# A two-layer hybrid decoder step on one core: running square sums in PSUM, unrolled residual loops, value pages loaded behind the output projection's weights

## The chip, the cores and the metric

The kernel runs on one core of a Trainium2 chip, in one launch. The metric is device time in microseconds (us). Before the change it is 1196.12 us, the median of three runs (1194.81 to 1197.56).

## The reference, cut to what matters

320 tokens (256 of a prompt, and 8 sequences of 8 new tokens) of width 1024 pass through two layers in float32. Cut to its core, a layer is:

```python
x = x + 0.5 * swiglu(rmsnorm(x, g1), w_gate1, w_up1, w_down1)      # 1024 -> 2816 -> 1024
z = rmsnorm(x, g) @ w_in                                           # 1024 -> 2048
q, k, v, p_in, c_in, d_in = split(z)
att  = moba_attention(q, concat(k_past, k), concat(v_past, v))     # past: pages picked by page_table
pool = pool_mixer(p_in)                                            # window means 2/4/8/16
conv = conv_module(c_in)                                           # GLU, depthwise 31, LayerNorm, swish
gmlp = spatial_gating(d_in)                                        # gelu, rmsnorm, causal mixing
x = x + concat(att, pool, conv, gmlp) @ w_out                      # 1024 -> 1024
x = x + 0.5 * swiglu(rmsnorm(x, g2), w_gate2, w_up2, w_down2)

def rmsnorm(x, gain):
    return x * rsqrt(mean(x * x, axis=-1) + 1e-6) * gain
```

The 8 sequences each have 256 past keys and values, two pages of 128 rows per sequence, whose place in the pool is read from `page_table` at run time.

## The kernel before

Channels lie on the 128 partitions and the 320 tokens along the free axis, so x is 8 tiles of 128 x 320 (`DT` = 8). Each weight is split into a rounded high part and a low rest, and so is each input; an output tile is the sum of three products (high by high, high by low, low by high), at lines L577, L578 and L580 of `use_slot`. For each input tile that is three matmuls of 128 x 128 by 320 columns.

The engines are programmed separately and meet at semaphores, in an order written out by hand. The outermost loop on each is over the two layers.

- **SyncE (SP)** issues the loads. Weights come in slots: four buffers `raw[j]`, each loaded at L347 (`load_slot`) once GpSimd has finished with its former content (semaphore `split`). In the input projection, SP waits until the FFN is done (its memory is reused), then goes through the last 8 of the 16 slots; behind each slot it loads the two pages of one sequence (`load_past`): per page it reads the page's number into a register, issues 128 KB of keys (L373) and 128 KB of values (L375). Both count on one semaphore, `kv_in`. Then come the 8 slots of the output projection, and those of the second FFN.
- **ScalarE (ACT)** rounds a slot to its high part `w_hi` (L885), as soon as it has landed and TensorE is done with the former slot in that place. In between it does the activations of the mixers, in a fixed order.
- **GpSimd (POOL)** subtracts to get the low part `w_lo` (L470). In the mixer stage, behind the last slot of the input projection, it also does the last 8 taps of the batch's convolution (`late_history_taps`, L488 and L491) and the sums of the pooling windows (`window_sums`, L506 to L533); only then it goes on to the slots of the output projection.
- **TensorE (PE)** runs the columns (24 matmuls, one output tile), and between the last columns of the input projection the small matmuls of the mixers. `batch_scores` (L700) reads the past keys and waits for `kv_in`; `batch_attention` (L787, L790), some 24 us later, reads the past values and has no wait for them of its own.
- **VectorE (DVE)** scales, does the taps of the convolution, the softmax's parts and all low parts of the inputs.

RMSNorm is applied late: the input of a matmul is x times the gain (`xg_hi` by ACT, L870; `xg_lo` by DVE, L1109), and the factor 1/rms multiplies the outputs. For it `residual` (L1151 on) does, for each of the 8 tiles of x: add the matmul's output to x (L1160), the low part `xg_lo` (L1109), and `add_square` (L1117), which adds the squares that ACT made (`square`, L877) to `sumsq` in SBUF. At the end one matmul with a matrix of ones (L620, `sum_squares`) sums over the partitions, ACT takes the root (L866), and `invert_norm` inverts it (L1121), sets `sumsq` to zero (L1122) and waits for its reciprocal. `residual` is a loop on the engine, of 2 tiles an iteration behind an FFN and of 4 behind the output projection. It runs three times a layer. Of the 8 PSUM banks, bank 7 holds the running sums of the convolution (`conv_sum`), later the conv statistics and one of the pooling maps.

Of the kernel before, what the change touches and what calls it, by code (L numbers as in the profile page):

```python
# [27 lines left out]
ALU = mybir.AluOpType  # L28
# [7 lines left out]
TOK = SEQ + NS  # L36
# [61 lines left out]
def hybrid_decoder(nc, xT, w8, w11, gains, vecs, consts, pool_w, conv_pw, sp_wT, sp_b,  # L98
# [3 lines left out]
    with ctx:  # L102
# [119 lines left out]
        kv_in = sig("kv_in", 16 * 2 * DEC_B * PAGES)  # L222
# [14 lines left out]
        summed = sig("summed", 3 * (DT + 1), DT + 1)  # L237
# [71 lines left out]

        conv_sum = bank[7][:, :].rearrange("p (c t) -> p c t", c=GT)  # L310
# [30 lines left out]
        def _(sp):  # L341
# [24 lines left out]
            def load_past(L, b):  # L366

                one = bass.ds(L, 1)
                for n in range(PAGES):
                    page = sp.value_load(page_row[0:1, bass.ds(b * PAGES + n, 1)],  # L370
                                         min_val=0, max_val=cache_v.shape[1] - 1)
                    at_page = bass.ds(page, 1)
                    sp.dma_start(k_all[:, :, bass.ds(b, 1), n * PAGE:(n + 1) * PAGE].rearrange("p c b t -> p c (b t)"),  # L373
                                 cache_kT[one, at_page, :, :, :].rearrange("l a p c t -> (l a p) c t")).then_inc(kv_in.sem, 16)
                    sp.dma_start(v_past[:, bass.ds(b * PAGES + n, 1), :].rearrange("p b t -> p (b t)"),  # L375
                                 cache_v[one, at_page, :, :].rearrange("l a p n -> (l a p) n")).then_inc(kv_in.sem, 16)
# [51 lines left out]
            with sp.Fori(0, DEPTH) as L:  # L428
# [10 lines left out]
                with sp.Fori(0, DEC_B // 4) as n:  # L439
                    for j in range(4):  # L440
                        load_slot(L, BASE_I, 2 + n, j, w8, L * W8_ROWS + (W8_I + 2) + n, HALVES8)
                        load_past(L, n * 4 + j)
                with sp.Fori(0, IT_O) as i:
                    load(L, BASE_O, i, w8, L * W8_ROWS + W8_O + i, HALVES8)
# [122 lines left out]
        def _(pe):  # L567
# [49 lines left out]
            def sum_squares(L, n):  # L617

                pe.wait_ge(summed.sem, L * summed.per + (n + 1) * (DT + 1))
# [72 lines left out]
            def batch_scores(L):  # L692
                pe.wait_ge(pads.sem, pads.at(L, 6))
                pe.wait_ge(kv_in.sem, kv_in.at(L, kv_in.per))
# [89 lines left out]
            def batch_attention(L):  # L784
                for g in range(2):
# [75 lines left out]
        def _(act):  # L861
# [69 lines left out]
            def norm_tile(L, tile0, norm, d, e):  # L931
                hold(act, taken.sem, L * taken.per + d + (tile0 + 1 + taken.head))
                norm_input(L * (3 * DT) + d + norm * DT, d, e, L * summed.per + d + norm * (DT + 1))
# [163 lines left out]
        def _(dve):  # L1097
# [16 lines left out]
            def add_square(squares, signal, tile_count, sum_count):  # L1114
                dve.wait_ge(signal.sem, tile_count + 1)
                dve.wait_ge(summed.sem, sum_count + 1)
                dve.tensor_tensor(sumsq[:, :], sumsq[:, :], squares, ALU.add).then_inc(summed.sem, 1)  # L1117

            def invert_norm(L, n):
                dve.wait_ge(norm_root.sem, norm_root.at(L, n + 1))  # L1120
                dve.reciprocal(rms[:, :], root[:, :]).then_inc(norm_ok.sem, 1)  # L1121
                dve.memset(sumsq[:, :], 0.0).then_inc(summed.sem, 1)  # L1122
# [28 lines left out]
            def residual(L, base, tile0, norm, factor, tiles_an_iteration, banks):  # L1151

                n_banks = len(banks)
# [384 lines left out]
```

## Time and profile before

| what | value |
|---|---|
| median of three runs | 1196.12 us (1194.81 to 1197.56) |
| the profiled execution | 1197.89 us, its span 1195.9 us |
| busy in the span | PE 1173.2 us (98%), DVE 623.4 us, ACT 547.8 us, POOL 814.4 us |
| mean granted TensorE clock | 0.995 of full speed |
| layer one, input projection and mixers | 245 to 339 us of the span |
| layer two, the same stage | 833 to 931 us of the span |

The profile is of one execution. "Busy" is the time in which an engine works on an instruction; matmuls overlap, one starts some 0.15 us after another and lasts 0.31 us, so PE's busy time shows where it stands still, and not how well it runs. The idle time in front of an instruction carries the name of what ended it. In the timeline that stands in square brackets; where there is none, the instruction followed at once.

### The profile page before, as it was taken

To read this page: it belongs to the slowest core of one execution; us is meant where nothing else is said; L and a number is where in the kernel's file an instruction comes from. 1 tells how busy PE (TensorE), PEld (TensorE's weight loads), DVE (VectorE), ACT (ScalarE), POOL (GpSimd) and SP (SyncE) were. 2 spreads that over 40 slices of the span, in tenths; PEclk is the share of its full clock that TensorE was granted. 3 is DMA by queue.
4 is the path that set the end of the run, shared out by engine and by line. 5 is a ranking of instruction groups with operands and counts; after the bars stand their busy time and mean duration, and the time that the engine had idled before them with its cause. 6 is when DMAs were issued, how large, how long until landed. Compare 5 with 4: busy or idle time off the path is not lost.

```text
span 1195.9 us, 24294 instructions
## 1 busy us (share of the span) xinstructions
PE 1173.2 (98%) x7924; PEld 1142.5 (96%) x7924; DVE 623.4 (52%) x913; ACT 547.8 (46%) x808; POOL 814.4 (68%) x427
## 2 busy tenths in 40 slices
PE   7999999999999999999999999999999999999998
PEld 6999999998789999999999999999986999999998
DVE  5775571247966444431157675522777664544212
ACT  5444444443845443444444444444455554443444
POOL 6776667675866767667767666677567566767677
PEclk9999999999999999999999999999998999999999
DMA  8454435566246544445555444455662364444455
GB/s 286 151 160 151 148 116 149 158 180 201 71 140 179 156 144 156 133 122 154 162 173 167 149 155 129 133 154 168 186 199 71 110 174 143 154 144 135 135 147 172
DMA packets 71831, 182.79 MB, mean 153 GB/s; under 512 B 10074, under 2 KB 24802, under 8 KB 71778
## 3 DMA queue, kind: packets, MB, share of 16 engines
q1 hardware_dynamic: 71488, 181.07, 49.7%
q10 hardware_dynamic: 290, 1.10, 0.2%
q8 instruction: 24, 0.39, 0.1%
q14 instruction: 29, 0.24, 0.1%
HBM read 178.55 MB, written 3.58 MB: 152 GB/s over the span
## 4 chain that ended last, share of the span: by engine, by line
PE 91%; DVE 5%; issue 1%; DMA 1%; ACT 1%; DVEq 0%; POOL 0%; SPq 0%; ACTq 0%
PE bank L577 29%; PE bank L580 29%; PE bank L578 29%; DVE xg_lo L1109 1%; DMA x<-in_xT 1%; DVE bank L1187 1%; PE bank L790 0%; PE bank L814 0%; PE bank L767 0%; DMA raw<-in_w 0%; PE bank L594 0%; PE bank L602 0%; PE bank L598 0%; PE bank L658 0%; DVE prob L1295 0%
## 5 line engine op out<-in xcount | busy, mean ns | idle before, releaser
L470 POOL TENSOR_TENSOR w_lo<-raw,w_hi 128x1024 fp32r<-128x1024 f32 (+2 forms) x353 | 767.7, 2179 | 360.3 <-ACT w_hi L885 360.1
L885 ACT ACTIVATE w_hi<-raw 128x1024 fp32r<-128x1024 f32 (+2 forms) x353 | 339.4, 962 | 471.0 <-PE bank L580 430.2
L577 PE MATMUL bank<-xg_hi,w_hi 128*128 128x320 f32 x1600 | 498.1, 311 | 5.1 <-DVE xg_lo L1109 4.2
L580 PE MATMUL bank<-xg_hi,w_lo 128*128 128x320 f32 x1600 | 494.9, 309 | 0.0
L578 PE MATMUL bank<-xg_lo,w_hi 128*128 128x320 f32 x1600 | 494.9, 309 | 0.0
L577 PEld LDWEIGHTS bank<-xg_hi,w_hi 128*128 128x128 f32 x1600 | 300.5, 188 | 10.0 <-DVE xg_lo L1109 5.3
L578 PEld LDWEIGHTS bank<-xg_lo,w_hi 128*128 128x128 f32 x1600 | 300.5, 188 | 0.6
L580 PEld LDWEIGHTS bank<-xg_hi,w_lo 128*128 128x128 f32 x1600 | 300.5, 188 | 0.0
L580 PE MATMUL bank<-h_hi,w_lo 128*128 128x320 f32 x704 | 217.8, 309 | 0.0
L577 PE MATMUL bank<-h_hi,w_hi 128*128 128x320 f32 x704 | 217.8, 309 | 0.0
L578 PE MATMUL bank<-h_lo,w_hi 128*128 128x320 f32 x704 | 217.8, 309 | 0.0
L1139 DVE TENSOR_TENSOR h_lo<-tmp,h_hi 128x320 f32 (+1 forms) x88 | 167.4, 1903 | 75.2 <-ACT h_hi L901 75.2
L577 PEld LDWEIGHTS bank<-h_hi,w_hi 128*128 128x128 f32 x704 | 132.2, 188 | 0.0
L578 PEld LDWEIGHTS bank<-h_lo,w_hi 128*128 128x128 f32 x704 | 132.2, 188 | 0.0
L580 PEld LDWEIGHTS bank<-h_hi,w_lo 128*128 128x128 f32 x704 | 132.2, 188 | 0.0
L1160 DVE SCALAR_TENSOR_TENSOR x<-bank,x 128x320 f32 x48 | 23.4, 487 | 203.1 <-PE bank L580 203.1
L1134 DVE TENSOR_TENSOR tmp<-bank,rms 128x320 f32<-128x320 f32 x88 | 43.1, 489 | 157.9 <-PE bank L580 157.8
L1109 DVE SCALAR_TENSOR_TENSOR xg_lo<-x,gain,xg_hi (+1 forms) x56 | 71.2, 1279 | 58.0 <-ACT xg_hi L870 58.0
L897 ACT ACTIVATE tmp<-tmp 128x320 f32<-128x320 f32 x88 | 40.7, 462 | 67.3 <-DVE tmp L1132 67.1
L1137 DVE TENSOR_TENSOR tmp<-tmp 128x320 f32<-128x320 f32 x88 | 57.3, 651 | 7.2 <-ACT tmp L897 4.7
L901 ACT ACTIVATE h_hi<-tmp 128x320 f32 (+1 forms) x88 | 41.5, 472 | 27.8 <-DVE tmp L1137 27.7
L1215 DVE SCALAR_TENSOR_TENSOR conv_y<-conv_in,vec,conv_y 128x64 f32<-128x64 f32 x88 | 46.7, 571 | 3.0
(180 smaller groups left out, 807.1 us busy)
## 6 DMA issues: line engine op xcount, KB each, us to landing
raw<-in_w SPq DMA_DIRECT2D x227, 512.0 KB, 3.8
raw<-in_w SPq DMA_DIRECT2D x64, 384.0 KB, 3.1
raw<-in_w SPq DMA_DIRECT2D x64, 320.0 KB, 2.9
k_all<-in_cache_kT SPq DMA_DIRECT2D x32, 128.0 KB, 2.9
v_past<-in_cache_v SPq DMA_DIRECT2D x32, 128.0 KB, 2.6
cst<-in_consts ACTq DMA_DIRECT2D x1, 997.0 KB
out_yT<-x SPq DMA_DIRECT2D x1, 960.0 KB, 7.4
x<-in_xT SPq DMA_DIRECT2D x2, 320.0 KB, 4.6
```

The source lines that it names most:

```text
L470: pool.tensor_tensor(w_lo[:, j, 0:count * P], raw[:, j, 0:count * P], w_hi[:, j, 0:count * P].bitcast(F32), ALU.subtract).then_inc(split.s ...
L577: pe.matmul(out, hi, in_hi[:, k, :], start=first and n == 0, stop=False)
L578: pe.matmul(out, hi, in_lo[:, k, :], start=False, stop=False)
L580: mm = pe.matmul(out, lo, in_hi[:, k, :], start=False, stop=last and end)
L885: act.activation(w_hi[:, j, 0:count * P], raw[:, j, 0:count * P], ACT.Copy).then_inc(split_hi.sem, 1)
L897: act.activation(tmp[:, 2 + m, :], tmp[:, m, :], ACT.Silu).then_inc(silu_ok.sem, 1)
L901: act.activation(h_hi[:, bass.ds(i * 2 + m, 1), :].rearrange("p a t -> p (a t)"), tmp[:, 6 + m, :], ACT.Copy).then_inc(h_hi_ok.sem, 1)
L1109: dve.scalar_tensor_tensor(out=xg_lo[:, bass.ds(d, 1), :].rearrange("p a t -> p (a t)"), in0=one, scalar=gain[:, bass.ds(gain_col, 1)], in ...
L1134: dve.tensor_tensor(tmp[:, 4 + m, :], bank[2 * m + 1][:, 0:TOK], rms[:, :], ALU.mult).then_inc(taken.sem, 1)
L1137: dve.tensor_tensor(tmp[:, 6 + m, :], tmp[:, 2 + m, :], tmp[:, 4 + m, :], ALU.mult).then_inc(h_ok.sem, 1)
L1139: dve.tensor_tensor(h_lo[:, bass.ds(i * 2 + m, 1), :].rearrange("p a t -> p (a t)"), tmp[:, 6 + m, :], h_hi[:, bass.ds(i * 2 + m, 1), :].b ...
L1215: dve.scalar_tensor_tensor(out=y, in0=window, scalar=weight, in1=y, op0=ALU.mult, op1=ALU.add).then_inc(batch_taps.sem, 1)
```

## The change

There are three parts.

1. **Running square sums in PSUM.** `add_square` gets the tile's number. For the first tile it copies the squares to bank 7, for the next six it adds them to bank 7, and for the last it adds bank 7 and the squares into `sumsq` in SBUF, which the matmul of ones reads as before. So nothing has to be zeroed, and the memset in `invert_norm` goes. The semaphore `summed` counts 8 instead of 9 a norm.
2. **Unrolled loops.** `residual` writes out its 8 tiles in place of a loop on the engine. It is still run three times in each of the two layers.
3. **Loads.** Behind each of the 8 slots of the input projection only the keys' two pages are loaded (semaphore `k_in`). The values' 16 pages go behind the first 4 slots of the output projection, 4 pages to a slot (`v_in`), and each page's number is read into a register a second time for them. `batch_scores` waits for `k_in`, and `batch_attention` gets a wait for `v_in`.

```diff
@@ -219,7 +219,8 @@
         half_in = sig("half_in", 0)
         raw_in = [sig(f"raw{j}_in", 16 * ITS) for j in range(4)]
         small_in = sig("small_in", 16 * SMALLS)
-        kv_in = sig("kv_in", 16 * 2 * DEC_B * PAGES)
+        k_in = sig("k_in", 16 * DEC_B * PAGES)
+        v_in = sig("v_in", 16 * DEC_B * PAGES)
         states_out = sig("states_out", 16 * STATES, 16)
         y_out = sig("y_out", 0)
         passed = sig("passed", 0)
@@ -234,7 +235,7 @@
         squared = sig("squared", 3 * DT)
         squared_first = sig("squared_first", 0)
         squared_too = sig("squared_too", 0)
-        summed = sig("summed", 3 * (DT + 1), DT + 1)
+        summed = sig("summed", 3 * DT, DT)
         norm_sum = sig("norm_sum", 3)
         norm_root = sig("norm_root", 3)
         norm_ok = sig("norm_ok", 3)
@@ -307,6 +308,7 @@
         mix_ok = sig("mix_ok", 9)
 
 
+        square_sum = bank[7][:, 0:TOK]
         conv_sum = bank[7][:, :].rearrange("p (c t) -> p c t", c=GT)
 
 
@@ -363,17 +365,21 @@
                     sp.dma_start(dst[:, :, :], src[one, :, :, :].rearrange("a p c n -> (a p) c n")).then_inc(small_in.sem, 16)
                 sp.dma_start(b_sp[:, :], sp_b[one, :, :].rearrange("a g t -> (a g) t")).then_inc(small_in.sem, 16)
 
-            def load_past(L, b):
-
-                one = bass.ds(L, 1)
+            def page_of(b, n):
+                return bass.ds(sp.value_load(page_row[0:1, bass.ds(b * PAGES + n, 1)],
+                                             min_val=0, max_val=cache_v.shape[1] - 1), 1)
+
+            def load_keys(L, b):
+
                 for n in range(PAGES):
-                    page = sp.value_load(page_row[0:1, bass.ds(b * PAGES + n, 1)],
-                                         min_val=0, max_val=cache_v.shape[1] - 1)
-                    at_page = bass.ds(page, 1)
                     sp.dma_start(k_all[:, :, bass.ds(b, 1), n * PAGE:(n + 1) * PAGE].rearrange("p c b t -> p c (b t)"),
-                                 cache_kT[one, at_page, :, :, :].rearrange("l a p c t -> (l a p) c t")).then_inc(kv_in.sem, 16)
+                                 cache_kT[bass.ds(L, 1), page_of(b, n), :, :, :].rearrange("l a p c t -> (l a p) c t")).then_inc(k_in.sem, 16)
+
+            def load_values(L, b):
+
+                for n in range(PAGES):
                     sp.dma_start(v_past[:, bass.ds(b * PAGES + n, 1), :].rearrange("p b t -> p (b t)"),
-                                 cache_v[one, at_page, :, :].rearrange("l a p n -> (l a p) n")).then_inc(kv_in.sem, 16)
+                                 cache_v[bass.ds(L, 1), page_of(b, n), :, :].rearrange("l a p n -> (l a p) n")).then_inc(v_in.sem, 16)
 
             def store_tokens(L, dst, src):
 
@@ -439,9 +445,12 @@
                 with sp.Fori(0, DEC_B // 4) as n:
                     for j in range(4):
                         load_slot(L, BASE_I, 2 + n, j, w8, L * W8_ROWS + (W8_I + 2) + n, HALVES8)
-                        load_past(L, n * 4 + j)
-                with sp.Fori(0, IT_O) as i:
-                    load(L, BASE_O, i, w8, L * W8_ROWS + W8_O + i, HALVES8)
+                        load_keys(L, n * 4 + j)
+                for j in range(4):
+                    load_slot(L, BASE_O, 0, j, w8, L * W8_ROWS + W8_O, HALVES8)
+                    load_values(L, 2 * j)
+                    load_values(L, 2 * j + 1)
+                load(L, BASE_O, 1, w8, L * W8_ROWS + (W8_O + 1), HALVES8)
                 load_and_store(L)
                 with sp.Fori(3, IT_G) as i:
                     load(L, BASE_G2, i, w8, L * W8_ROWS + W8_G2 + i, HALVES8)
@@ -616,7 +625,7 @@
 
             def sum_squares(L, n):
 
-                pe.wait_ge(summed.sem, L * summed.per + (n + 1) * (DT + 1))
+                pe.wait_ge(summed.sem, L * summed.per + (n + 1) * DT)
                 pe.matmul(bank[6][:, 0:TOK], ones[:, :], sumsq[:, :], start=True, stop=True).then_inc(norm_sum.sem, 1)
 
             def column(L, base, tile0, norm, i, j, first=False):
@@ -691,7 +700,7 @@
 
             def batch_scores(L):
                 pe.wait_ge(pads.sem, pads.at(L, 6))
-                pe.wait_ge(kv_in.sem, kv_in.at(L, kv_in.per))
+                pe.wait_ge(k_in.sem, k_in.at(L, k_in.per))
                 for g in range(2):
                     pe.wait_ge(p_biased.sem, p_biased.at(L, 6 + 2 * g))
                     for b4 in range(4):
@@ -782,6 +791,7 @@
                                  ident).then_inc(s_tr.sem, 1)
 
             def batch_attention(L):
+                pe.wait_ge(v_in.sem, v_in.at(L, v_in.per))
                 for g in range(2):
                     pe.wait_ge(s_copied.sem, s_copied.at(L, 2 * g + 2))
                     pe.matmul(bank[2 + g][:, 0:GT * P], prob_nt[:, g, :], v_tok_s[:, :], start=True, stop=False, skip_group_check=True)
@@ -930,7 +940,7 @@
 
             def norm_tile(L, tile0, norm, d, e):
                 hold(act, taken.sem, L * taken.per + d + (tile0 + 1 + taken.head))
-                norm_input(L * (3 * DT) + d + norm * DT, d, e, L * summed.per + d + norm * (DT + 1))
+                norm_input(L * (3 * DT) + d + norm * DT, d, e, L * summed.per + d + (norm * DT - 1))
 
             def down(L, base, tile0, norm, last):
 
@@ -1111,15 +1121,18 @@
                                          in1=xg_hi[:, bass.ds(d, 1), :].bitcast(F32).rearrange("p a t -> p (a t)"),
                                          op0=ALU.mult, op1=ALU.subtract).then_inc(xg_lo_ok.sem, 1)
 
-            def add_square(squares, signal, tile_count, sum_count):
-                dve.wait_ge(signal.sem, tile_count + 1)
-                dve.wait_ge(summed.sem, sum_count + 1)
-                dve.tensor_tensor(sumsq[:, :], sumsq[:, :], squares, ALU.add).then_inc(summed.sem, 1)
+            def add_square(d, squares, square_count, sum_count):
+
+                dve.wait_ge(squared.sem, square_count + 1)
+                if d == 0:
+                    dve.tensor_copy(square_sum, squares).then_inc(summed.sem, 1)
+                else:
+                    dve.wait_ge(summed.sem, sum_count)
+                    dve.tensor_tensor(sumsq[:, :] if d == DT - 1 else square_sum, square_sum, squares, ALU.add).then_inc(summed.sem, 1)
 
             def invert_norm(L, n):
                 dve.wait_ge(norm_root.sem, norm_root.at(L, n + 1))
                 dve.reciprocal(rms[:, :], root[:, :]).then_inc(norm_ok.sem, 1)
-                dve.memset(sumsq[:, :], 0.0).then_inc(summed.sem, 1)
                 hold(dve, norm_ok.sem, norm_ok.at(L, n + 1))
 
             def gate_up_step(L, base, tile0, ffn, i):
@@ -1150,17 +1163,13 @@
 
             def residual(L, base, tile0, norm, factor, tiles_an_iteration, banks):
 
-                n_banks = len(banks)
-                with dve.Fori(0, DT // n_banks) as i:
-                    for e in range(n_banks):
-                        d = i * n_banks + e
-                        slots_a_tile = 4 // tiles_an_iteration
-                        dve.wait_ge(slots.sem, L * slots.per + d * slots_a_tile + (4 * base + slots_a_tile + slots.head))
-                        one = x[:, bass.ds(d, 1), :].rearrange("p a t -> p (a t)")
-                        dve.scalar_tensor_tensor(out=one, in0=bank[banks[e]][:, 0:TOK], scalar=factor, in1=one,
-                                                 op0=ALU.mult, op1=ALU.add).then_inc(taken.sem, 1)
-                        input_rest(L * (3 * DT) + d + norm * DT, d, L * (3 * DT) + d + norm * DT)
-                        add_square(square[:, e % 2, :], squared, L * (3 * DT) + d + (norm - 1) * DT, L * summed.per + d + norm * (DT + 1))
+                slots_a_tile = 4 // tiles_an_iteration
+                for d in range(DT):
+                    dve.wait_ge(slots.sem, L * slots.per + d * slots_a_tile + (4 * base + slots_a_tile + slots.head))
+                    dve.scalar_tensor_tensor(out=x[:, d, :], in0=bank[banks[d % len(banks)]][:, 0:TOK], scalar=factor, in1=x[:, d, :],
+                                             op0=ALU.mult, op1=ALU.add).then_inc(taken.sem, 1)
+                    input_rest(L * (3 * DT) + d + norm * DT, d, L * (3 * DT) + d + norm * DT)
+                    add_square(d, square[:, d % 2, :], L * (3 * DT) + d + (norm - 1) * DT, L * summed.per + d + norm * DT)
 
             for n, piece in enumerate(X_PIECES):
                 dve.wait_ge(x_in[n].sem, 16)
@@ -1170,7 +1179,7 @@
                 dve.tensor_tensor(tmp[:, d, :], x[:, d, :], x[:, d, :], ALU.mult).then_inc(squared_too.sem, 1)
             dve.wait_ge(squared_first.sem, DT // 2)
             dve.wait_ge(squared_too.sem, DT // 2)
-            dve.tensor_reduce(sumsq[:, :], tmp[:, :, :].rearrange("p d t -> p t d"), AX.X, ALU.add).then_inc(summed.sem, DT + 1)
+            dve.tensor_reduce(sumsq[:, :], tmp[:, :, :].rearrange("p d t -> p t d"), AX.X, ALU.add).then_inc(summed.sem, DT)
 
             def take(L, t, dst, b=None):
 
```

## Rows read from the trace of the kernel before

**Rows 1.** The page's busy times by engine, with share of the span and instructions.
```profile
PE 1173.2 (98%) x7924; PEld 1142.5 (96%) x7924; DVE 623.4 (52%) x913; ACT 547.8 (46%) x808; POOL 814.4 (68%) x427
```
**Rows 2.** PE's waits: who waited for whom, total us, times, longest.
```profile
PE bank L577 <- DVE xg_lo L1109: 4.2, 4, 1.2
```
**Rows 3.** Timeline, first step of layer one: start, us, engine, line, operation, [idle before].
```profile
26.36 0.33 DVE L1122 MEMSET sumsq<- 128x320 f32 x1
26.60 0.48 DVE L1132 TENSOR_TENSOR tmp<-bank,rms 128x320 f32<-128x320 f32 x1
...
27.22 0.41 PE L577 MATMUL bank<-xg_hi,w_hi 128*128 128x320 f32 x1 [0.82 <-DVE tmp L1132]
```
**Rows 4.** Groups by line, DVE: count, busy us, mean ns, idle before.
```profile
L1187 DVE SCALAR_TENSOR_TENSOR bank<-conv_in,vec,bank 128x256 f32<-128x256 f32 x116 | 46.5, 483 | 0.3 <-DVE bank L1187 0.3
...
L1117 DVE TENSOR_TENSOR sumsq<-sumsq,square 128x320 f32<-128x320 f32 x48 | 23.0, 479 | 0.0
```
**Rows 5.** Timeline, from the FFN to the input projection, layer one.
```profile
242.50 7.12 POOL L470 TENSOR_TENSOR w_lo<-raw,w_hi 128x1024 fp32r<-128x1024 f32 x3 [0.24 <-ACT w_hi L885]
...
247.45 2.51 DVE L1109 SCALAR_TENSOR_TENSOR xg_lo<-x,gain,xg_hi  x1 [1.08 <-ACT xg_hi L870]
...
249.89 0.48 DVE L1117 TENSOR_TENSOR sumsq<-sumsq,square 128x320 f32<-128x320 f32 x1
...
250.56 0.70 PE L620 MATMUL bank<-sumsq,ones 128*128 128x320 f32 x2
```
**Rows 6.** Timeline of SP's issues in the input projection, layer one.
```profile
261.03 0.34 SPq L347 DMA_DIRECT2D raw<-in_w  x1
262.38 0.58 SPq L373 DMA_DIRECT2D k_all<-in_cache_kT  x1
263.17 0.47 SPq L375 DMA_DIRECT2D v_past<-in_cache_v  x1
...
266.11 0.34 SPq L347 DMA_DIRECT2D raw<-in_w  x1
```
**Rows 7.** Timeline, the projection's last slot on PE, ACT, DVE and POOL, layer one.
```profile
292.12 0.31 PE L580 MATMUL bank<-xg_hi,w_lo 128*128 128x320 f32 x1
...
295.39 0.41 DVE L1287 COPY q_pad<-qk 64x64 f32<-64x64 f32 x2
...
297.11 1.06 ACT L885 ACTIVATE w_hi<-raw 128x1024 fp32r<-128x1024 f32 x1 [4.52 <-DMA raw<-in_w]
...
298.25 2.36 POOL L470 TENSOR_TENSOR w_lo<-raw,w_hi 128x1024 fp32r<-128x1024 f32 x1 [3.24 <-ACT w_hi L885]
...
324.92 9.79 POOL L470 TENSOR_TENSOR w_lo<-raw,w_hi 128x1024 fp32r<-128x1024 f32 x4
```
**Rows 8.** Timeline, softmax scaling and PE's wait behind it, layers one and two.
```profile
311.36 2.58 DVE L1321 TENSOR_TENSOR prob<-prob,stat 128x512 f32<-128x512 f32 x2
...
317.59 0.66 PE L683 MATMUL bank<-cst,z_v 128*128 128x128 f32 x4 [0.70 <-DVE z_v L1178]
...
898.93 3.16 DVE L1321 TENSOR_TENSOR prob<-prob,stat 128x512 f32<-128x512 f32 x2
...
905.74 0.66 PE L683 MATMUL bank<-cst,z_v 128*128 128x128 f32 x4 [1.06 <-DVE z_v L1178]
```
**Rows 9.** Timeline, the batch's softmax, its readers on PE, two low parts.
```profile
320.76 0.45 DVE L1345 TENSOR_TENSOR prob_new<-prob_s,cst 128x128 f32<-128x128 f32 x1
...
322.40 0.44 PE L780 MATMUL bank<-cst,prob_s 128*128 128x128 f32 x2
...
917.40 4.93 DVE L1361 TENSOR_TENSOR mix_lo<-tmp,mix_hi 128x320 fp32r<-128x320 f32 x2
```
**Rows 10.** Stretch by stretch: us, busy by engine, granted clock, DMA share, GB/s.
```profile
915.00:920.00 5.00, 5.00 (x28) 2.52 (x27) 3.00 (x3) 2.03 (x4) 5.00 (x3) 0.50 0.57 165
```
**Rows 11.** Timeline, the pooling map on PE, layers one and two.
```profile
333.57 1.24 PE L807 MATMUL bank<-tmp,w_pool 128*128 128x320 f32 x4
...
926.15 1.24 PE L807 MATMUL bank<-tmp,w_pool 128*128 128x320 f32 x4
```

## The prediction

> **What bounds the kernel now.** I read the busy times first. PE works through 98% of the span [rows 1], and where it works it runs at one pace, so only what makes PE stand still can move the time, and the clock. So the next view is the list of PE's waits. Of these the change touches three places: the last low part of x behind `residual`, which comes last 4 times for 4.2 us in all [rows 2], the first step of the first FFN (0.82 us, [rows 3]), and the mixers, where PE waits 0.70 us in layer one and 1.06 us in layer two for the last of DVE's outputs [rows 8]. Third, the timelines of SP, ACT, POOL and DVE around these places, and last the granted clock: it stood at half (0.50, the 1.2 GHz level) from about 915 us, in layer two's mixers [rows 10]. From the same matmul to the same matmul PE needed 333.57 - 317.59 = 15.98 us in layer one and 926.15 - 905.74 = 20.41 us in layer two [rows 8, 11], so this fall cost 4.4 us. That is more than any edit below is worth.
>
> **The memset** (0.33 us, 6 times). It matters where the reciprocal's reader is late: in the first step DVE starts the output 0.24 us behind the memset's start, and PE waited for that output [rows 3]. Without it PE starts some 0.22 us earlier. In layer two the same three instructions open the layer and PE's wait is too short to be listed, so there it is 0 to -0.22 us. In the other norms PE has three more columns to do first. I take -0.3 us in all.
>
> **The sums in PSUM.** 48 adds of 0.48 us in SBUF [rows 4] become 36 adds in the bank, 6 copies into it and 6 adds from it to SBUF. An add with PSUM on both sides shows as the convolution's tap, 0.48 us at 256 columns; at 320 this is at most 0.60 us. So an add costs between 0 and 0.12 us more. Seven of eight lie in the time of the next tile's matmuls. The last is read by the matmul of ones: it ended at 250.37 us and that matmul began at 250.56 [rows 5], so 0.19 us of cover hides the 0.12. Were it dearer, what goes beyond 0.19 would count in the four norms inside the layers. Nor does the wait for the low part shrink: this instruction was issued at 247.45 us and ended at 249.96, 0.34 us behind the end (242.50 + 7.12 = 249.62) of POOL's run [rows 5]. It has both inputs in SBUF, and was held until POOL's instruction was over; the adds come behind it. I take 0.
>
> **The unrolled loops.** The same instructions are issued in the same order. A loop's branch lies between two tiles, where DVE waits for PE's matmuls; behind the last tile there is nothing but the loop's exit. I take 0, between -0.4 us (0.1 us for each exit where the sum is read next, less than the 0.19 us that stand between) and 0; the cover is PE's own columns.
>
> **The keys alone behind the input projection's slots.** SP needs 5.08 us from slot to slot (261.03 to 266.11, [rows 6]), of which each of the two value pages takes 0.47 us and the 0.21 us in front of it. Without them it is 3.7 us. Seven such periods lie ahead of the last slot, so its load may go out up to 9.5 us earlier. ACT waited 4.52 us for that slot [rows 7], and this wait goes. What is late next is the place in `w_hi`: PE ends the column before at 292.12 + 0.31 = 292.43 us, so ACT starts at 292.6 in place of 297.11, and POOL's last low part of the projection is over at 296.1 in place of 300.6. PE gains nothing by it: no wait of PE names these slots. But POOL's late taps and window sums follow at once, and so they, and the four low parts of the output projection's slots behind them (from 324.92 us), come 4.5 us earlier: these start at 320.4. POOL's instructions then meet others of DVE.
>
> First, the softmax scaling (L1321, two instructions). By the add's pace, 0.48 us for 320 elements, I estimate that they need 1.65 us for 512 and 1024; they took 2.58 and 3.16 [rows 8], that is 0.9 and 1.5 us of waiting for POOL's window sums. In the new order they still meet them, at another phase: the wait can be anything from 0 to about 1.9 (two of POOL's instructions). PE's next wait takes over the difference, from -0.70 to +1.0 us in layer one and from -1.06 to +0.4 in layer two. Since the two layers show two phases of this already, I take their mean again: 0.
>
> Second, the batch's softmax. L1345 ran from 320.76 to 321.21 us, and PE read its result at 322.40 [rows 9]. If POOL's first low part (9.79 / 4 = 2.45 us, [rows 7]) starts at 320.4 and gets in ahead, L1345 ends at 320.4 + 2.45 + 0.15 = 323.0 and PE starts 0.7 us late; if DVE gets in first, nothing is lost. I take +0.2 us a layer, +0.4 in all. The far end: DVE's two low parts L1361, issued while POOL ran four low parts in a row, took 4.93 us [rows 9], one full wait each. If L1345 and the scaling ahead of it both lose like this, it is 2.45 us more, +3.1 a layer.
>
> A copy of DVE (L1287, 0.2 us, at 295.39 us, [rows 7]) would also run beside POOL's low part that now ends at 296.1; no row shows a copy beside a busy POOL, so it costs between 0 and 0.7 us a layer, and I take 0, as its single input comes nearer to the taps, which nothing held up [rows 4]. The Trainium skill ("SBUF — State Buffer", Who interferes with whom) speaks against that: a float32 copy inside SBUF can take the port pair that DVE shares with GpSimd, and then waits for GpSimd's whole instruction. By that rule the sum would be 1.4 us higher. Its other half, that two inputs in SBUF contend, the trace bears out (the 2.51 us above).
>
> **The values behind the output projection's slots, and the new wait.** A slot and four pages, with a register read for each page, take SP up to about 6.5 us (today a slot and four loads take 5.08). The first such slot went out about one period behind the one that ACT got at 297.11, whose load I put 5 us ahead of that; so at about 297.2, and 9.5 us earlier now. Four slots end at 287.7 + 26 = 314 us, and the data land by some 318. The new wait stands on PE ahead of `batch_attention`, behind L780 at 322.40 [rows 9]; so 4 us of cover, and 0. If the loads came later than that, all of PE's rest of the stage would be behind the wait. The output projection's slots are split only behind POOL's window sums, so they are not missed either.
>
> **The sum.** -0.3 + 0 + 0 + 0 + 0.4 + 0 = +0.1 us. On the profiled execution that is 1197.89 (2.0 of it outside the span) to 1198.0; the median of the runs is 1.8 us lower, so 1196.2 us. For this kernel, 0.2% or 2.4 us is about what can be told from no change: 1193.7 to 1198.5.
>
> **The rivals.**
>
> *The clock doesn't fall in layer two (faster).* Both layers do the same work in this stage and only layer two fell, after the longer of two short waits (1.06 against 0.70 us). If the scaling meets POOL at a better phase there, the fall may stay out: 1196.2 - 4.4 = 1191.8 us. Against it: the rest of PE's work in that stretch, small matmuls, is as it was.
>
> *It falls in layer one too (slower).* The same from the other side, if PE waits longer than 0.70 us there: 1196.2 + 4.4 = 1200.6. The Trainium skill ("TensorE: Matmul & The Clock Gate", What's actually happening) says that the clock follows how busy the array has lately been; by that rule every wait added in the mixers makes this likelier. One fall in two like stages is all that the trace shows of it.
>
> *POOL's earlier low parts hold up DVE (slower).* The place is L1345 and the scaling in front of it, the price one or two waits of 2.45 us less the 1.2 us of cover, and it decides when POOL's run starts before DVE's instruction is issued (320.4 against 320.76, so close). One wait in both layers: +1.4 - 0.3, 1197.2 us, still no change; two waits in both: +6.2 - 0.3, 1202 us; in one layer: about 1199.
>
> *The loads don't make the slots earlier.* SP's load also waits until POOL has freed the slot; if that holds it, POOL's work stays where it is and only the memset is left: 1195.8 us.
>
> **Chances.** The forecast, with the loads' rival beside it (same answer): 0.57, its own range 1194.0 to 1198.4. No fall: 0.16. A second fall: 0.11. DVE held up beyond one wait: 0.12. The rest, 0.04, on either side. Faster by over 0.2%: 0.16 + 0.05 from the forecast's lower edge (both waits of PE gone, -1.8, and the memset) = 0.21; slower: 0.11 + 0.12 + 0.02 = 0.25; same 0.54. The range leaves out half of each far case: 1191.8 to 1200.2.
>
> **What would show it.** Right: no memset, ACT's last slot of the projection without a wait for its load, POOL's first low part of the output projection near 320 us, 4 to 5 us earlier than before; PE's wait for `z_v` between 0 and 1.9 us; no wait of PE for `v_past`; the matmul of ones without a wait. Wrong: a wait of PE in front of L780 or L787, a new wait at L620, or another number of falls of the clock; with the latter the time leaves the forecast's range whatever the edits do.

## The result, and the profile after

The changed kernel takes 1208.55 us (median of 11 runs, 1198.7 to 1210.71) against 1195.19 us of the kernel before beside it (11 runs, 1193.98 to 1197.95): 1.0103 times as long, 95% interval 1.0085 to 1.0120. I had forecast 1196.2, no change that could be told, and the range ended at 1200.2. Lines of code after the change are 9 to 13 further down than before (L780 is now L789, L1345 is L1354, L470 is L479).

The profiled execution took 1208.05 us (span 1205.9). The first view is from the list of TensorE's waits in it: who waited for whom, us in total, times, longest.

```profile
PE bank L586 <- DVE xg_lo L1119: 4.2, 4, 1.2
PE bank L789 <- DVE prob_new L1354: 2.9, 2, 1.4
...
PE bank L692 <- DVE z_v L1187: 2.4, 2, 1.3
...
PE bank L740 <- ACT tmp L1045: 0.7, 1, 0.7
PE bank L586 <- DVE tmp L1145: 0.4, 1, 0.4
```

The low parts of x cost 4.2 us as before [rows 2]; the first step's wait is 0.4 us here and was 0.82 before [rows 3], which the section on the prediction takes up. The waits on `z_v` sum to 2.4 us and were 1.8 before (0.70 and 1.06, [rows 8]). New are the wait on `prob_new`, once in each layer, and a short one at L740. The next view is the timeline of the changed kernel around `prob_new` (start, us, engine, line, operation, [idle before]); the first rows are layer one, the last three layer two.

```profile
319.38 10.05 POOL L479 TENSOR_TENSOR w_lo<-raw,w_hi 128x1024 fp32r<-128x1024 f32 x4
...
319.69 0.15 DVE L1348 RECIPROCAL stat<-stat 128x2 f32<-128x2 f32 x1
...
319.88 2.67 DVE L1350 TENSOR_TENSOR prob_s<-prob_s,stat 128x528 f32<-128x528 f32 x1
...
322.59 2.33 DVE L1354 TENSOR_TENSOR prob_new<-prob_s,cst 128x128 f32<-128x128 f32 x1
...
324.97 0.44 PE L789 MATMUL bank<-cst,prob_s 128*128 128x128 f32 x2 [1.45 <-DVE prob_new L1354]
...
914.94 7.74 POOL L479 TENSOR_TENSOR w_lo<-raw,w_hi 128x1024 fp32r<-128x1024 f32 x3
...
918.14 2.33 DVE L1354 TENSOR_TENSOR prob_new<-prob_s,cst 128x128 f32<-128x128 f32 x1
...
920.52 0.44 PE L789 MATMUL bank<-cst,prob_s 128*128 128x128 f32 x2 [1.43 <-DVE prob_new L1354]
```

Before, POOL's low parts began at 324.92 us, behind `prob_new` (320.76) [rows 7, 9], and the scaling ahead of it was short:

```profile
319.86 0.86 DVE L1341 TENSOR_TENSOR prob_s<-prob_s,stat 128x528 f32<-128x528 f32 x1
```

Now POOL's low parts begin at 319.38, half a microsecond ahead of the scaling (now L1350). That instruction and L1354 behind it last 2.67 and 2.33 us, near one low part of POOL each (10.05 / 4 = 2.5); they took 0.86 and 0.45 us before [rows 9]. The same happens in layer two.

The third view is the stretches of 5 us: us, busy time of PE, PE's weight loads, DVE, ACT, POOL, then the granted clock, the DMA share and GB/s.

```profile
320.00:325.00 5.00, 3.56 (x36) 2.75 (x34) 4.96 (x3) 3.25 (x8) 5.00 (x3) 1.00 0.29 88
325.00:330.00 5.00, 5.00 (x28) 3.12 (x28) 4.96 (x4) 2.72 (x6) 4.43 (x2) 0.91 0.61 198
330.00:335.00 5.00, 5.00 (x27) 2.55 (x27) 2.62 (x7) 3.34 (x6) 0.00 (x0) 0.50 0.43 137
335.00:340.00 5.00, 5.00 (x24) 2.44 (x24) 0.00 (x0) 0.62 (x2) 0.00 (x0) 0.57 0.00 0
...
920.00:925.00 5.00, 4.48 (x22) 2.91 (x22) 4.96 (x4) 2.73 (x6) 4.98 (x3) 0.80 0.63 197
925.00:930.00 5.00, 5.00 (x20) 2.71 (x22) 3.03 (x8) 3.31 (x5) 0.00 (x0) 0.50 0.50 166
930.00:935.00 5.00, 5.00 (x38) 2.29 (x31) 0.14 (x1) 0.77 (x2) 0.00 (x0) 0.67 0.00 0
```

Behind the wait the granted clock is at half (0.50, 1.2 GHz) in both layers; before, only in layer two [rows 10]. The price of this is read on TensorE alone, from the matmul behind `z_v` to the pooling map:

```profile
318.84 0.66 PE L692 MATMUL bank<-cst,z_v 128*128 128x128 f32 x4 [1.06 <-DVE z_v L1187]
...
340.76 1.24 PE L817 MATMUL bank<-tmp,w_pool 128*128 128x320 f32 x4
...
914.40 0.66 PE L692 MATMUL bank<-cst,z_v 128*128 128x128 f32 x4 [1.34 <-DVE z_v L1187]
...
936.21 1.24 PE L817 MATMUL bank<-tmp,w_pool 128*128 128x320 f32 x4
```

That is 21.92 and 21.81 us, where the kernel before needed 15.98 without a fall and 20.41 with one [rows 8, 11]. 15.98, a wait of 1.45 and a fall of 4.4 make 21.83. The two profiled executions differ here by 5.94 us in layer one and 1.40 in layer two, 7.3 of the 10.2 us between them (1208.05 - 1197.89). Over the 11 runs the time goes with the mean granted clock (correlation -0.93, 957 us for 1.0 of clock): 0.998 in the shortest run (1198.7 us), 0.987 in the two at 1210.2 and 1210.3.

### The profile page after: what moved, and what is told of

The parts are those of the page before. It is cut to its first block, busy times and chain, and to the rows that moved or that the text cites. A ratio compares the mean times of both kernels' runs of the same rounds, so it can differ in the third digit from the quotient of the medians.

```text
span 1205.9 us, 24214 instructions
## 1 busy us (share of the span) xinstructions
PE 1180.0 (98%) x7924; PEld 1147.0 (95%) x7924; DVE 630.6 (52%) x907; ACT 547.1 (45%) x808; POOL 813.9 (67%) x427
## 4 chain that ended last, share of the span: by engine, by line
PE 86%; DVE 7%; issue 4%; ACT 1%; DMA 1%; DVEq 1%; POOL 0%; SPq 0%; ACTq 0%
PE bank L586 27%; PE bank L589 27%; PE bank L587 27%; ACT xg_hi L880 1%; DVE xg_lo L1119 1%; DVE x L1169 1%; DMA x<-in_xT 1%; PE bank L800 1%; DVE bank L1196 1%; PE bank L776 1%; DVE bank L1131 0%; PE bank L824 0%; DVE prob_s L1350 0%; DMA raw<-in_w 0%; PE bank L603 0%
## 5 line engine op out<-in xcount | busy, mean ns | idle before, releaser
L479 POOL TENSOR_TENSOR w_lo<-raw,w_hi 128x1024 fp32r<-128x1024 f32 (+2 forms) x353 | 767.8, 2180 | 371.6 <-ACT w_hi L895 371.3
L1169 DVE SCALAR_TENSOR_TENSOR x<-bank,x 128x320 f32<-128x320 f32 x48 | 23.3, 486 | 199.2 <-PE bank L589 199.2
L1119 DVE SCALAR_TENSOR_TENSOR xg_lo<-x,gain,xg_hi 128x320 fp32r<-128x320 f32 x56 | 75.0, 1346 | 57.4 <-ACT xg_hi L880 57.4
```

The costliest lines, as they stand in the source:

```text
L479: pool.tensor_tensor(w_lo[:, j, 0:count * P], raw[:, j, 0:count * P], w_hi[:, j, 0:count * P].bitcast(F32), ALU.subtract).then_inc(split.s ...
L1119: dve.scalar_tensor_tensor(out=xg_lo[:, bass.ds(d, 1), :].rearrange("p a t -> p (a t)"), in0=one, scalar=gain[:, bass.ds(gain_col, 1)], in ...
```

## The experiments

The order of loads was one suspect (A), the sums and the written-out loops the other (B); C stands for some of each. For the falls of the clock there were two theories: that TensorE's waits bring them (W), or something else in the changed kernel (D, V). All runs are compared with the kernel before on the same chip.

**1. The loads alone.** The kernel before, with only this of the change:

```diff
-                        load_past(L, n * 4 + j)
-                with sp.Fori(0, IT_O) as i:
-                    load(L, BASE_O, i, w8, L * W8_ROWS + W8_O + i, HALVES8)
+                        load_keys(L, n * 4 + j)
+                for j in range(4):
+                    load_slot(L, BASE_O, 0, j, w8, L * W8_ROWS + W8_O, HALVES8)
+                    load_values(L, 2 * j)
+                    load_values(L, 2 * j + 1)
+                load(L, BASE_O, 1, w8, L * W8_ROWS + (W8_O + 1), HALVES8)
```

> The kernel before with the new order of loads alone: keys behind the last eight slots of the input projection, values behind the first four of w_out, the two semaphores; the sums of squares stay in SBUF with their memset, and the loops stay loops. Theory A (order of loads): GpSimd's taps, window sums and first four w_out low parts come some 5 us earlier and meet VectorE's copies and the batch's softmax; TensorE waits 3 to 4 us longer, and the clock falls more often. It expects about 1208 us (1203 to 1211), and the new wait of TensorE on prob_new (some 1.4 us in each layer). Theory B (sums and unrolling): the PSUM sums or the written-out loops cost the time; it expects 1195 us. Theory C (each part some): between, about 1200 us.

Measured: 1205.87 us, 1.0101 (1.0075 to 1.0128). The wait is there again, from TensorE's waits of this run and from its timeline (layer one, then layer two):

```profile
PE bank L788 <- DVE prob_new L1354: 2.9, 2, 1.4
```

```profile
319.09 0.66 PE L691 MATMUL bank<-cst,z_v 128*128 128x128 f32 x4 [1.07 <-DVE z_v L1187]
...
325.21 0.44 PE L788 MATMUL bank<-cst,prob_s 128*128 128x128 f32 x2 [1.44 <-DVE prob_new L1354]
...
336.38 1.24 PE L816 MATMUL bank<-tmp,w_pool 128*128 128x320 f32 x4
...
909.81 0.66 PE L691 MATMUL bank<-cst,z_v 128*128 128x128 f32 x4 [0.81 <-DVE z_v L1187]
...
915.94 0.44 PE L788 MATMUL bank<-cst,prob_s 128*128 128x128 f32 x2 [1.44 <-DVE prob_new L1354]
...
931.73 1.24 PE L816 MATMUL bank<-tmp,w_pool 128*128 128x320 f32 x4
```

The wait is the same in both layers, and the clock fell behind it in layer two only: from `z_v` to the pooling map TensorE needs 17.29 us in layer one and 21.92 in layer two.

**2. Everything but the loads.** The changed kernel with the loads of before (the diff above, reversed).

> The changed kernel with the loads as before (each slot of the input projection followed by two key pages and two value pages, one semaphore). Sums in PSUM and written-out loops stay. Theory A expects 1194.5 to 1195.5 us: before, less some 0.3 us of the memset. Theory B expects about 1208 us. Theory C about 1203 us.

Measured: 1195.74 us, 1.0005 (0.9992 to 1.0017). So the sums, the missing memset and the loops make no difference that can be told, and the loads make the whole loss: A stands, B and C fall.

**3. POOL's low parts held back.** The changed kernel with a wait in front of the `w_out` slots:

```diff
+                hold(pool, s_norm.sem, s_norm.at(L, 3))
                 with pool.Fori(0, IT_O) as i:
                     split_iteration(L, BASE_O, i, HALVES8)
```

> The changed kernel, with one wait more on GpSimd: the w_out low parts don't begin until VectorE has written prob_new. Taps and window sums keep their early place, and so meet VectorE's copies as in the changed kernel. Theory A: the two softmax products fall back to 0.86 and 0.45 us, the wait on prob_new (2.9 us over both layers) goes; what is left is the copies' loss in the input projection (about 1 us a layer) and the falls of the clock that follow from it. It expects 1197 to 1203 us. Theory D (the clock falls in the changed kernel for another reason than these waits, such as the transfers' new order): the direct wait alone goes, 1205 to 1206 us, with as many stretches at a granted clock under 0.9.

Measured: 1197.29 us, 1.0024 (1.0007 to 1.0040). The two products on its timeline:

```profile
320.07 0.71 DVE L1351 TENSOR_TENSOR prob_s<-prob_s,stat 128x528 f32<-128x528 f32 x1
320.81 0.29 DVE L1355 TENSOR_TENSOR prob_new<-prob_s,cst 128x128 f32<-128x128 f32 x1
```

They are short again, no wait on `prob_new` is listed, and from `z_v` to the pooling map TensorE needs 15.77 and 15.78 us (319.04 to 334.81, 909.99 to 925.77): no fall there in either layer of this profile. Of the 13.4 us lost, 2.9 are left: one wait of an engine that has time to spare takes back some 10 us, more than three times the 2.9 us that the waits on `prob_new` themselves cost. D, which expected 1205, falls.

**4. POOL's taps held back too**, to where they were before, with all loads in the new order:

```diff
+                hold(pool, taps.sem, taps.at(L, 2 * 26))
                 hold(pool, batch_taps.sem, batch_taps.at(L, batch_taps.per))
```

> The changed kernel, with one wait more on GpSimd: the late taps don't begin until VectorE has done its prompt taps to the 26th (52 of 62), which puts taps, window sums and the w_out low parts back to within about 1 us of their times in the kernel before, while all loads keep the new order. Theory A expects 1194.5 to 1197 us: the copies at 0.20 us, no wait on prob_new, the falls as before. Theory D, and any theory in which the transfers themselves cost the time, expects 1205 to 1209 us.

Measured: 1194.99 us, 1.0006 (0.9994 to 1.0019). The loads themselves, their order, the register reads and the new wait of TensorE for the values cost nothing that can be told. What cost the time was only when POOL works.

**5. The wait without the loads.** Does TensorE's wait bring the falls, or does something around it? The kernel before, with two instructions on VectorE that nobody reads:

```diff
+                dve.reciprocal(root[:, :], rms[:, :])
+                dve.reciprocal(square[:, 0, 0:88], rms[:, 0:88])
                 dve.wait_ge(s_norm.sem, s_norm.at(L, 2))
                 dve.tensor_tensor(prob_new[:, :, :, :],
```

> The kernel before, with two reciprocals that nobody reads on VectorE just ahead of prob_new (128x320 and 128x88, together some 2.75 us): prob_new ends as late against TensorE as in the changed kernel, and GpSimd, the loads and the sums are those of before. Theory W (a wait of TensorE in the mixer makes the clock fall behind it): the wait on prob_new comes back at some 1.4 us a layer, and the time is about 1194.5 + 2.9 of waits + some 8 of clock, 1203 to 1207 us, with a stretch at a granted clock near 0.5 behind it in both layers. Theory V (the falls have another cause in the changed kernel, such as what the transfers or GpSimd do there): the direct wait alone, 1197 to 1198 us.

Measured: 1201.56 us, 1.0058 (1.0036 to 1.0079). The line of its waits, and two stretches of layer two:

```profile
PE bank L780 <- DVE prob_new L1347: 2.7, 2, 1.6
```

```profile
920.00:925.00 5.00, 5.00 (x25) 2.04 (x23) 4.87 (x6) 1.91 (x4) 4.74 (x2) 0.50 0.60 197
925.00:930.00 5.00, 5.00 (x26) 2.79 (x26) 0.10 (x1) 0.38 (x1) 0.00 (x0) 0.64 0.46 148
```

It lies below W's range and above V's. 7.1 us are lost for 2.7 us of waiting; in this profile the clock fell in layer two, behind a wait of 1.05 us, and not in layer one, behind one of 1.62. One of the six runs had the full clock throughout (1.000) and took 1195.96 us, the other five had 0.989 to 0.995. So the wait makes a fall likelier, and doesn't make it certain.

**6. The wait, with TensorE busy in it.** The changed kernel, with three matmuls that nobody reads, ahead of the wait:

```diff
-                pe.wait_ge(s_norm.sem, s_norm.at(L, 3))
                 pe.wait_ge(gm_copied.sem, gm_copied.at(L, 2))
                 pe.wait_ge(cv_rt.sem, cv_rt.at(L, 1))
+                for n in range(3):
+                    pe.matmul(bank[7][:, 0:TOK], ones[:, :], rms[:, :], start=True, stop=True)
+                pe.wait_ge(s_norm.sem, s_norm.at(L, 3))
```

> The changed kernel, with three fp32 matmuls of 128x320 (some 1.6 us) that nobody reads on TensorE just ahead of its wait for prob_new: the softmax is as late as in the changed kernel, but TensorE is busy while it waits. Theory W expects the falls behind this place to go: the time falls from about 1207 to 1198 to 1201 us although the batch's probabilities come no earlier. Theory V expects no change, 1205 to 1209 us.

Measured: 1200.03 us, 1.0057 (1.0038 to 1.0075). Its timeline and stretches behind the place in layer one (each of the three matmuls shows as two, as the one of L620 does in [rows 5]):

```profile
323.63 2.33 DVE L1356 TENSOR_TENSOR prob_new<-prob_s,cst 128x128 f32<-128x128 f32 x1
...
324.51 1.88 PE L787 MATMUL bank<-rms,ones 128*128 128x320 f32 x6
```

```profile
325.00:330.00 5.00, 5.00 (x28) 3.11 (x26) 4.97 (x4) 2.73 (x7) 5.00 (x3) 1.00 0.64 195
330.00:335.00 5.00, 5.00 (x49) 2.74 (x48) 3.58 (x8) 3.47 (x6) 0.47 (x1) 1.00 0.63 196
```

`prob_new` still takes 2.33 us and TensorE still can't go on earlier (`z_v` to the pooling map is 17.44 us in each layer, 1.46 over the 15.98), yet the clock stays at 1.00 in both layers. Over the kernel before it is 5.6 us, in place of 13.4: some 8 us are won, nearly the two falls of 4.4. The mean clock of its six runs is 0.997, against 0.991 of the changed kernel's; two of the six, at 0.994, took 1203.75 and 1204.58 us, so not every fall is kept out. For this place W holds and V falls: with the batch's softmax as late as before, TensorE's standing idle is what most of the falls there need.

**7. POOL held in both places, but its taps only behind the copies.**

```diff
+                hold(pool, pads.sem, pads.at(L, 6))
                 hold(pool, batch_taps.sem, batch_taps.at(L, batch_taps.per))
...
+                hold(pool, s_norm.sem, s_norm.at(L, 3))
                 with pool.Fori(0, IT_O) as i:
```

> The changed kernel with two waits more on GpSimd: the late taps don't begin until VectorE has done its copies of q and k (some 2 us later than in the changed kernel, 3 earlier than before), and the w_out low parts don't begin until prob_new is written. Theory A: both places of loss go, 1194 to 1196 us, as with the taps held until the 26th. If it is not the copies but the taps and window sums against VectorE's other work that made the 2.3 us which were left with the low parts held alone, it stays at 1197 us.

Measured: 1196.62 us, 1.0024 (1.0013 to 1.0034), so the copies were not what was left: in layer one they take 0.86 and 0.40 us here, just as in experiment 4. Two rows of layer one:

```profile
311.05 0.80 DVE L1324 TENSOR_SCALAR stat<-stat 128x2 f32<-128x2 f32 x1
```

```profile
318.21 0.66 PE L694 MATMUL bank<-cst,z_v 128*128 128x128 f32 x4 [1.70 <-DVE z_v L1189]
```

An instruction of two elements in a partition took 0.80 us beside the earlier window sums (0.39 and 0.17 in the two layers of the kernel before), and TensorE's wait on `z_v` was 1.70 us, against 1.07 in each layer of experiment 4. That doesn't make the 1.6 us between the two experiments: in layer two of experiment 7 no such wait is listed, and its sum is the smaller one (experiment 7, then 4):

```profile
PE bank L694 <- DVE z_v L1189: 1.7, 1, 1.7
```

```profile
PE bank L693 <- DVE z_v L1188: 2.1, 2, 1.1
```

The mean clock of the runs is a little lower here (median 0.9955 against 0.997); why, stays open.

**8. TensorE kept busy in the wait of the kernel before.**

```diff
             def value_rows(L):
+                pe.wait_ge(taken.sem, taken.at(L, T_I + 14))
+                for n in range(2):
+                    pe.matmul(bank[1][:, 0:TOK], ones[:, :], rms[:, :], start=True, stop=True)
                 pe.wait_ge(taken.sem, taken.at(L, T_O))
```

> The kernel before, with two fp32 matmuls of 128x320 (some 1.07 us) that nobody reads on TensorE just ahead of its wait for z_v, 1.1 us long in its profile. Theory W: this wait is behind the fall that the kernel before has in layer two (clock 0.50 from 914.6 to 924.9); with the array busy it goes, and the time is 1192.5 to 1193.5 us, with less spread. Theory V expects 1194.4 us, or up to 0.6 us more where the two matmuls outlast the wait.

Measured: 1194.56 us, 0.9998 (0.9989 to 1.0008). The mean clock is 0.998 in all but two of 11 runs and higher in those, and the runs lie within 2.7 us (1193.05 to 1195.78) where the 23 runs of before lie within 5.8; but the median doesn't move. In layer two the added matmuls held TensorE until 906.94 us, while `z_v` was there at 906.12, so they put off what follows; and most runs of the kernel before have no long fall to lose (next section).

**9 and 10. A shorter wait.** VectorE's reciprocal ahead of `z_v` cut in two, alone and with the sums in PSUM:

```diff
-                dve.reciprocal(gm_root[:, :], gm_root[:, :]).then_inc(gm_v.sem, 1)
+                half = TOK // 2
+                dve.reciprocal(gm_root[:, 0:half], gm_root[:, 0:half]).then_inc(gm_v.sem, 1)
                 take(L, 15, z_v[:, 1, :])
-                dve.wait_ge(gm_v.sem, gm_v.at(L, 1))
+                dve.reciprocal(gm_root[:, half:TOK], gm_root[:, half:TOK]).then_inc(gm_v.sem, 1)
+                dve.wait_ge(gm_v.sem, gm_v.at(L, 2))
```

> The kernel before, with VectorE's reciprocal of the gate norm's root (2.14 us) cut into two halves of 160 columns, and z_v's second part taken between them instead of behind the whole. Theory W expects that TensorE's wait on z_v (1.06 us in each layer of the profile) nearly goes and one of about 0.6 us on the scaled gates z_w comes in its place, so about 0.4 us a layer is won directly, and with shorter waits the clock falls less often: 1192.5 to 1193.8 us. Theory V (this wait is harmless) expects 1193.5 to 1194.4 us. If the cut costs VectorE more than some 0.2 us, or the scaled gates come later, it is 1194.5 to 1195.5 us.

> The same cut with the sums of squares in PSUM and the written-out loops, and the loads as before: the version that would beat both kernels if both pieces are worth their estimates. Theory W: 1192 to 1193.8 us, as the cut alone, less some 0.3 us of the memset. If the sums and loops are worth nothing or a little loss, as their own run left open (1.0005, interval 0.9992 to 1.0017), it equals the cut alone within 0.6 us.

Measured: 1193.55 us, 0.9994 (0.9984 to 1.0004), and 1193.87 us, 0.9998 (0.9988 to 1.0007): no version here is measurably faster than the kernel before. Two rows of experiment 9 set a bound to W. In its profiled execution, the longest of 13 (1200.84 us), no wait on `z_v` is listed any more, TensorE was busy throughout, and the clock fell all the same in layer one:

```profile
320.00:325.00 5.00, 5.00 (x45) 3.56 (x43) 4.90 (x9) 4.27 (x11) 4.19 (x8) 1.00 0.01 3
...
330.00:335.00 5.00, 5.00 (x32) 2.04 (x36) 5.00 (x3) 0.85 (x2) 4.73 (x2) 0.50 0.72 220
```

## Why the prediction was wrong

**The memset** was put at -0.3 us and was worth nothing. The reciprocal and the output behind it, in the kernel before (its output L1132 starts at 26.60 [rows 3]) and in the changed one:

```profile
24.19 2.15 DVE L1121 RECIPROCAL rms<-root 128x320 f32<-128x320 f32 x1 [4.12 <-ACT root L866]
```

```profile
23.58 2.15 DVE L1135 RECIPROCAL rms<-root 128x320 f32<-128x320 f32 x1 [4.12 <-ACT root L876]
...
25.97 0.49 DVE L1145 TENSOR_TENSOR tmp<-bank,rms 128x320 f32<-128x320 f32 x1 [0.24 <-DVE rms L1135]
```

Without the memset VectorE stands idle for 0.24 us until its own reciprocal is done, a wait that the memset had filled: from one start to the other it is 2.39 us now and was 2.41 before. TensorE's wait at this step is no longer with the memset than without it (experiment 2, without; experiment 1, with):

```profile
PE bank L578 <- DVE tmp L1136: 0.8, 1, 0.8
```

```profile
PE bank L585 <- DVE tmp L1141: 0.3, 1, 0.3
```

So the step from 0.82 to 0.44 us in the changed kernel is not the memset's doing.

**The sums and the unrolled loops** at 0: borne out by experiment 2. An add in the bank takes 0.49 us, as in SBUF (0.48, [rows 4]), so the upper bound of 0.12 us more did not come up (shortest, median and longest, in ns):

```profile
L1131 DVE TENSOR_TENSOR bank<-bank,square x36: 484/486/489, 189.7 to 1194.1; 128x320 f32<-128x320 f32 x36
```

**The chain of loads** was right. ACT's last slot of the projection waits for TensorE and not for its load, and starts at 291.82 (forecast 292.6); POOL's late taps start at 295.29 instead of 300.56, its first low part of `w_out` at 319.38 (forecast 320.4), 5.5 us earlier than before. The last value pages were issued by 309.5 us (forecast 314). TensorE has no wait for `v_past`, and experiment 4 shows that the loads themselves cost nothing that can be told.

**The step that failed** is the batch's softmax: "I take +0.2 us a layer". The forecast start, 320.4 us, lay between the issues of the two products; the true one, 319.38, lay ahead of both. So each waited out a low part of POOL, in both layers, which is the prediction's own far end and its third rival. The term hung on half a microsecond, and the estimate of the start was 1 us off; it should have had a far larger chance than 0.12. The price of the far end was put too high: TensorE waited 1.45 us a layer, not 3.1, because VectorE was ahead by then (the gates' scaling in front, L1344, took 1.06 us where it had met POOL for 2.29 before).

**The wait for `z_v`**, put at 0, grew to 1.06 and 1.34 us, 0.6 us more over both layers and inside the stated bounds. It didn't come by way of the scaling that I had looked at: in the changed kernel this took 2.18 us in each layer, against 2.58 and 3.16 before [rows 8]. By the add's pace it needs 2.3 us (0.48 x 1536 / 320), not the 1.65 that I wrote, so less of it had been waiting. What else held VectorE up was not traced.

**What was left out** was larger. The third rival priced two waits in both layers at 1202 us, and the second fall of the clock stood as a rival of its own, at 0.11. But the one makes the other likely. An estimate from the profiles: to the 1195.2 us of the kernel before, two waits on `prob_new` (2.9) and the longer ones on `z_v` and at L740 (2.4 - 1.8 + 0.7 = 1.3) give 1199.4, near the shortest run of the changed kernel (1198.7, at a clock of 0.998); two falls of 4.4 more give 1208.2, against the median of 1208.55. Experiments 3, 5 and 6 show the tie from three sides. It is a tie of chances: over the twelve profiles, six mixer stages have TensorE idle for 1.05 to 1.62 us before `prob_new` (the changed kernel, experiments 1 and 5), and the clock fell in four of them; of the other 18 it fell in two (layer two of the kernel before, layer one of experiment 9). The Trainium skill ("TensorE: Matmul & The Clock Gate", What's actually happening) has the clock follow how busy the array has lately been. Experiment 6, where the array was kept busy and the granted clock stayed at 1.00, agrees. I had cited this section of the Trainium skill and then given the waits and the fall a chance each, as though the two were independent.

**The copies**, taken at 0, were held up too: in layer one 1.00 and 0.68 us for pairs that took 0.41 and 0.40 before [rows 7].

```profile
292.95 2.38 POOL L479 TENSOR_TENSOR w_lo<-raw,w_hi 128x1024 fp32r<-128x1024 f32 x1 [1.11 <-ACT w_hi L895]
...
294.75 1.00 DVE L1296 COPY q_pad<-qk 64x64 f32<-64x64 f32 x2
...
295.29 0.41 POOL L497 TENSOR_TENSOR tmp<-conv_in,vec 128x128 f32<-128x128 f32 x1
```

The Trainium skill ("SBUF — State Buffer", Who interferes with whom), whose rule I had set aside here, was right that a copy, with its single input, can contend: the 1.00 us lie beside the end of POOL's low part and its first tap. My argument that a copy is nearer to the taps was wrong. Between experiments 3 (copies at 1.00 and 0.68 us) and 7 (0.86 and 0.40) the time differs by 0.7 us at most, so their own price stays below what can be told.

**The fall of the kernel before** was misread as fixed. The profiled execution that I started from had one, and a mean clock of 0.995. Of 75 runs of this kernel beside the experiments the median is 0.998, and 14 have 0.995 or less; by the changed kernel's 957 us for 1.0, a fall of 4.4 us is some 0.0046 of clock. So its usual run has no long fall, there was little of it to win (experiments 8 to 10), and what the first rival waited for is already so in most runs.

## What to carry to other kernels

An engine off the critical path that is let go earlier is not free: look up which instructions of other engines it will then run beside, and hold it with one wait if they slow each other down; here that wait was worth some 10 of 13 us. Price a wait of TensorE in a stretch of small matmuls together with the fall of the clock that it may bring (here 4.4 us behind a wait of 1.45, in four stages of six), as one case and not as two. Where such a wait can't be removed, matmuls that nobody reads can keep the clock up: in experiment 6 they won some 8 us, in experiment 8, where they outlasted a shorter wait, nothing. And before an instruction is priced as saved, look whether the engine would have waited in its place, as it does here for its reciprocal.

## What was not expected of the hardware

Matmuls whose results nobody reads kept the granted clock at 1.00 through a wait that without them (1.45 and 1.43 us in the changed kernel's profile) was followed by a fall in both layers. A fall needs no listed wait (experiment 9's profile), so waits change how often it comes, and what starts one is open. The short falls around 295 us (granted 0.66 from 295 to 300 in the changed kernel, 0.74 in experiment 2, whose time is that of before) were not looked into.
